# MLP gate and up products by Strassen's scheme, down products behind all of them, zero-state products dropped

## The chip, the cores and the metric

The kernel runs on one core of one Trainium2 chip. The core has TensorE (matmuls into PSUM), VectorE, ScalarE and GpSimd (element-wise work), SyncE (which mostly issues DMA transfers), 16 DMA engines, an on-chip SBUF and a PSUM of 8 banks of 512 float32 columns. The metric is the device time of one launch in microseconds.

## The reference, cut to what matters

A stack of three blocks over `x` (1024 tokens x 1024 features, float32): an S5 and a gMLP block, an SSD and retention block with an MLP, and an mLSTM and long convolution block. The change is in the second and third:

```python
    # second block: y_ssd and y_ret come from chunked scans, 8 chunks of 128 tokens
    x = x + jnp.einsum("bse,ed->bsd", mixed, w_out[i])
    h = rmsnorm_2(x, norm2_w[i])
    a = jax.nn.silu(jnp.einsum("bsd,df->bsf", h, w_gate[i]))   # 1024 -> 2816
    u = jnp.einsum("bsd,df->bsf", h, w_up[i])                  # 1024 -> 2816
    x = x + jnp.einsum("bsf,fd->bsd", a * u, w_down[i])        # 2816 -> 1024

def chunk_state_scan(states, decay):
    def step(carry, inp):
        s, d = inp
        return (carry * d + s).astype(carry.dtype), carry
    _, prev = lax.scan(step, jnp.zeros_like(states[0]), (states, decay))
    return prev
```

The mLSTM of the third block carries its state `C` from zero over 8 chunks in the same way. In all three mixers the state that the first chunk reads is zero, and nothing reads the state that the last chunk leaves.

## The kernel before

Activations lie turned, features on the 128 partitions and the 1024 tokens in a row, as 8 slices (`KT`) in `XT`. Every projection is worked out one tile of 128 output features at a time. Both operands are split into a high and a low part of a shorter float format, and three products are summed in PSUM (high x high, high x low, low x high): a tile is 8 slices x 3 parts x 2 token halves = 48 matmuls 128x512, all in `pe_tile` (L445), with the two buffers `PP[0]` and `PP[1]` in turns. GpSimd splits the weights (`split_tile`, L412 and L415), SyncE loads them (`load_tile`, L382), ScalarE and VectorE split the activations into `Hhi`, `Hlo` (`split_hi`, `split_lo`, L587, L594, L596). The order on each engine is written out by hand, and semaphores count finished tiles (`proj_done`), evicted tiles (`psum_free`), split weights (`w_split`) and split activation slices (`h_ready`).

The MLP runs in three groups of 8, 8 and 6 pairs. A pair is a gate tile and an up tile; VectorE evicts both times the norm's factor `nrs` (L2381, L2383), ScalarE applies Silu, VectorE multiplies (L2386), and the result is split into one slice of `AUhi`, `AUlo`. After each group its part of the down product is added to `XT` (8 tiles, `add_tile`, L530). The norm before it (`norm2`) is deferred: tiles of `gu0` start on `XT` times the norm's weight, and the factor of each token is worked out beside them. `add_deferred` is the last stretch of VectorE's work before:

```python
            for k in range(KT):
                if k == KT - 1:
                    low_halves(range(KT // 2))
                add_tile(dve, name, k // 2, k % 2, subchunks=subchunks)
                dve.drain().then_inc(hf_ready, 1)
                if k == KT - 1:
                    low_halves(range(KT // 2, KT))
                square_add(dve, b, k)
```

In the mixers, TensorE's products of a chunk stand between quarters of projection tiles (`part`) so that it has work while VectorE and ScalarE turn a chunk around. In the mLSTM stage VectorE also runs the long convolution, one step of 1.3 us (L1100) per tap and slice, spread over the chunks by `CONV_SLOTS`. After it, `convb_sync`, `convb_pe`, `convb_dve` and `convb_act` run the `ya` projection (its operand `mlstm` comes back from DRAM) beside the norm of the convolution.

## Time and profile before

| | us |
|---|---|
| median of 3 runs | 3804.71 (3803.73 to 3807.9) |
| the profiled execution | 3802.75 |
| its span, first to last instruction | 3801.0 |
| TensorE busy | 3609.1 (95%) |
| VectorE busy | 2117.7 (56%) |
| GpSimd busy | 1013.7 (27%) |
| ScalarE busy | 924.4 (24%) |
| mean granted clock of TensorE | 0.977 of full |

Busy times are shares of the whole span. Successive matmuls overlap in the records, so the time that one costs is the distance between starts, not its own duration. A float32 matmul that isn't of the shorter format shows as two records.

### The profile page before, as it was taken

What the parts mean: (1) busy time and instruction counts of PE and PEld (TensorE: products, weight loads), DVE (VectorE), ACT (ScalarE), POOL (GpSimd) and SP (SyncE); (2) the same over time, 40 slices, a digit from 0 to 9 for tenths busy, and PEclk for the clock granted to TensorE, in tenths of its full rate; (3) what the DMA queues carried; (4) which work ended last, traced back from release to release, by engine and by line L of the source; (5) the groups of instructions that cost most, each with busy time, mean ns of one, the idle gap of its engine ahead of it and who ended that gap; (6) DMA issues with size and microseconds to landing.
All of it is one profiled execution on the core that took longest, in us unless ns stands there. A gap on an engine that the chain in (4) does not pass through costs nothing.

```text
span 3801.0 us, 44173 instructions
## 1 busy us (share of the span) xinstructions
PE 3609.1 (95%) x17330; PEld 2959.7 (78%) x17330; DVE 2117.7 (56%) x2154; ACT 924.4 (24%) x1027; POOL 1013.7 (27%) x457
## 2 busy tenths in 40 slices
PE   6888999999899999998999999999999999998998
PEld 4677888887687887776888888887778888876886
DVE  7687551265762664545421221246469888866646
ACT  3355221121122332311210000113332222224222
POOL 0000443333243322332444444433100000004442
PEclk9899999999899999999999999999999999999998
DMA  3234313352125765643111111114433555563521
GB/s 127 68 90 129 100 49 111 105 162 76 34 79 155 174 159 142 175 113 111 45 50 48 46 50 50 44 49 131 150 128 128 165 161 161 150 199 128 177 94 61
DMA packets 540019, 415.59 MB, mean 109 GB/s; under 512 B 33480, under 2 KB 496712, under 8 KB 539872
## 3 DMA queue, kind: packets, MB, share of 16 engines
q1 hardware_dynamic: 478320, 293.94, 28.1%
q10 hardware_dynamic: 61552, 119.65, 8.4%
q8 instruction: 98, 1.61, 0.2%
q14 instruction: 49, 0.40, 0.0%
HBM read 291.00 MB, written 120.16 MB: 108 GB/s over the span
## 4 chain that ended last, share of the span: by engine, by line
PE 85%; DVE 7%; ACT 2%; DVEq 2%; DMA 2%; issue 1%; SPq 0%; ACTq 0%; POOL 0%; POOLq 0%
PE proj_ps L445 74%; ACT stage L473 1%; DVE Hlo L594 1%; PE mix_ps L1460 1%; DVE AUX L677 1%; PE proj_ps L1471 1%; DVE WORK L1100 0%; PE proj_ps L2171 0%; PE mix_ps L660 0%; DVEq L675 0%; PE mix_ps L698 0%; PE proj_ps L2172 0%; PE mix_ps L2267 0%; PE mix_ps L2186 0%; PE proj_ps L1324 0%
## 5 line engine op out<-in xcount | busy, mean ns | idle before, releaser
L445 PE MATMUL proj_ps<-Hhi,w_hi 128*128 128x512 f32 x4128 | 1321.4, 402 | 117.1 <-DVE Hlo L594 60.4
L445 PE MATMUL proj_ps<-Hlo,w_hi 128*128 128x512 f32 x4128 | 1285.1, 393 | 0.0
L445 PE MATMUL proj_ps<-Hhi,w_lo 128*128 128x512 f32 x4128 | 1281.2, 392 | 0.0
L412 POOL TENSOR_TENSOR w_hi<-w_raw,zero_col 128x1024 fp32r<-128x1024 f32 (+2 forms) x225 | 429.9, 1911 | 2712.6 <-PE proj_ps L445 1577.8
L445 PEld LDWEIGHTS proj_ps<-Hhi,w_hi 128*128 128x128 f32 x4128 | 768.9, 190 | 314.1 <-issue 84.6
L445 PEld LDWEIGHTS proj_ps<-Hhi,w_lo 128*128 128x128 f32 x4128 | 781.2, 189 | 167.5
L445 PEld LDWEIGHTS proj_ps<-Hlo,w_hi 128*128 128x128 f32 x4128 | 781.8, 189 | 166.7
L415 POOL TENSOR_TENSOR w_lo<-w_raw,w_hi 128x1024 fp32r<-128x1024 f32 (+2 forms) x225 | 581.7, 2585 | 32.0
L1100 DVE SCALAR_TENSOR_TENSOR WORK<-WORK,param_cols 128x1024 f32<-128x1024 f32 x240 | 308.3, 1285 | 20.2 <-issue 0.9
L473 ACT ACTIVATE stage<-proj_ps 128x1024 f32<-128x1024 f32 x112 | 130.2, 1163 | 597.0 <-PE proj_ps L445 596.0
L530 DVE TENSOR_TENSOR XT<-XT,proj_ps 128x1024 f32<-128x1024 f32 (+1 forms) x64 | 78.1, 1220 | 328.0 <-PE proj_ps L445 328.0
L2383 DVE TENSOR_TENSOR AUX<-proj_ps,AUX 128x1024 f32<-128x1024 f32 x22 | 27.0, 1225 | 205.5 <-PE proj_ps L445 205.5
L689 ACT ACTIVATE AUX<-XT 128x1024 f32<-128x1024 f32 (+1 forms) x47 | 49.9, 1062 | 336.9 <-DVE XT L530 311.3
L445 PE MATMUL proj_ps<-AUlo,w_hi 128*128 128x512 f32 x352 | 109.8, 393 | 0.0
L445 PE MATMUL proj_ps<-AUhi,w_hi 128*128 128x512 f32 x352 | 109.1, 391 | 0.0
L445 PE MATMUL proj_ps<-AUhi,w_lo 128*128 128x512 f32 x352 | 108.7, 390 | 0.0
L2372 ACT ACTIVATE AUX<-AUX 128x1024 f32<-128x1024 f32 x22 | 23.4, 1062 | 339.1 <-DVE AUX L2381 339.1
L486 DVE TENSOR_TENSOR stage<-proj_ps,AUX 128x1024 f32<-128x1024 f32 x24 | 29.4, 1225 | 134.4 <-PE proj_ps L445 132.3
L540 DVE TENSOR_TENSOR AUX<-AUX 128x1024 f32<-128x1024 f32 x31 | 80.9, 2611 | 31.9 <-ACT AUX L689 31.7
L594 DVE TENSOR_TENSOR Hlo<-WORK,Hhi 128x1024 fp32r<-128x1024 f32 x56 | 84.1, 1534 | 25.4 <-ACT Hhi L587 17.2
L402 DVE TENSOR_TENSOR w_lo<-w_raw,w_hi 128x1024 fp32r<-128x1024 f32 x64 | 78.1, 1222 | 19.8 <-ACT w_hi L396 16.5
L2381 DVE TENSOR_TENSOR AUX<-proj_ps,AUX 128x1024 f32<-128x1024 f32 x22 | 27.0, 1225 | 105.3 <-PE proj_ps L445 105.1
(436 smaller groups left out, 3449.7 us busy)
## 6 DMA issues: line engine op xcount, KB each, us to landing
w_raw<-in_w_in SPq DMA_DIRECT2D x101, 512.0 KB, 4.4
w_raw<-in_sgu_w_in SPq DMA_DIRECT2D x24, 512.0 KB, 3.8
w_raw<-in_w_out SPq DMA_DIRECT2D x24, 512.0 KB, 4.1
w_raw<-in_w_gate SPq DMA_DIRECT2D x22, 512.0 KB, 3.9
w_raw<-in_w_up SPq DMA_DIRECT2D x22, 512.0 KB, 3.8
w_raw<-in_s_w_in SPq DMA_DIRECT2D x16, 512.0 KB, 4.3
WORK<-mid_acs SPq DMA_DIRECT2D x8, 1024.0 KB, 17.2
mid_qkv<-stage ACTq DMA_DIRECT2D x16, 512.0 KB, 4.9
```

The costliest lines, as they stand in the source:

```text
L402: engine.tensor_tensor(wlo[slot][:, :, :], raw[slot][:, :, :], whi[slot][:, :, :].bitcast(F32), ALU.subtract)\
L412: nc.gpsimd.tensor_tensor(whi[slot][:, 0:kt, :], w, zero_col[:, 0:1].unsqueeze(2).to_broadcast([P, kt, P]), ALU.add)
L415: nc.gpsimd.tensor_tensor(wlo[slot][:, 0:kt, :], raw[slot][:, 0:kt, :], whi[slot][:, 0:kt, :].bitcast(F32), ALU.subtract).then_inc(w_split, 1)
L445: mm = nc.tensor.matmul(ps[:, h * HALF:(h + 1) * HALF], a[slot][:, k, :], b[:, at + k, h * HALF:(h + 1) * HALF], start=(k == 0 and n == 0) ...
L473: a = nc.scalar.activation(dst, src, func)
L530: nc.vector.tensor_tensor(x, x, o.unsqueeze(1), ALU.add).then_inc(psum_free, 1)
L540: nc.vector.tensor_tensor(nsq[0], nsq[0], nsq[1], ALU.add).then_inc(S("sq_added"), 1)
L594: m = nc.vector.tensor_tensor(dst, src, part.bitcast(F32), ALU.subtract)
L677: nc.vector.scalar_tensor_tensor(out=nhf[k % 2], in0=XT[:, k, :], scalar=g(k), in1=rstd, op0=ALU.mult, op1=ALU.mult)\
L689: nc.scalar.activation(nsq[1].unsqueeze(1), XT[:, ds(k, 1), :], ACT.Square).then_inc(S("sq_ready"), 1)
L1100: m = nc.vector.scalar_tensor_tensor(out=acc, in0=u[:, j:j + SEQ], scalar=col(f"convb_w{j}", k), in1=acc, op0=ALU.mult, op1=ALU.add)
L1460: mm = nc.tensor.matmul(o, k8(ml_qe)[:, 2 * h + d, :], cx(d, h), start=False, stop=(d == 1))
```

## The change

Each pair's gate and up tiles are taken as one product of a 2x2 block matrix of weights (gate and up by upper and lower half of the 1024 inputs) with a 2x2 block matrix of activations (upper and lower inputs by first and second 512 tokens). Strassen's scheme, in the form with seven products `P1` to `P7` and chained sums, computes it: each product is 4 slices x 3 parts = 12 matmuls 128x512. Three weight-side operands are taken as they are and four are sums (`block_sums`), worked out for every pair on VectorE; three activation-side operands are differences, worked out once per slice as out_ret's tiles finish (`first_difference`, `other_differences`) and held in `AUhi`, `AUlo`. ScalarE makes the high and VectorE the low part of each weight block, seven products ahead; GpSimd has no part in it. Intermediate sums stay in three PSUM banks per pair (two sets): ScalarE copies a bank after `P1`, `P6` and `P5`, and VectorE adds copies and banks after `P2`, `P5`, `P3` and `P4`. `P1` of a pair is moved ahead into the pair before. The result of each pair goes to DRAM (`au`) and is read back and split for the down products, which all stand behind the 22 pairs. In SSD, retention and mLSTM the products with the zero state in chunk 0 and the state update in the last chunk go; the remaining conv steps of the last mLSTM chunk stand behind its output, and SyncE's and VectorE's work around `ya` is in another order. Several semaphores are renamed, since they are now shared by two stages.

```diff
+AU_TILES = (8, 8, 6)
+PAIRS = sum(AU_TILES)
+
+ORDER = [(0, "P1"), (1, "P1")] + [(p, j) for p in range(PAIRS) for j in ("P2", "P6", "P7", "P5", "P1", "P3", "P4") if not (p == 0 and j == "P1")]
+ORDER = [(p + 1, j) if j == "P1" and n > 1 else (p, j) for n, (p, j) in enumerate(ORDER)]
+ORDER = [x for x in ORDER if x[0] < PAIRS]
+TURN = {x: n for n, x in enumerate(ORDER)}
 
 
...
-            for m, n in enumerate((8, 8, 6)):
-                proj(f"gu{m}", "w_gate_2", 0, m * D, 2 * n, "norm2", pair="w_up_2")
+            proj("gu", "w_gate_2", 0, 0, 2 * PAIRS, "norm2", pair="w_up_2")
+            for m, n in enumerate(AU_TILES):
                 h(f"au{m}", n)
+            for m, n in enumerate(AU_TILES):
                 proj(f"down{m}", "w_down_2", 0, 0, 8, f"au{m}", kt=n, row0=m * D)
         if 3 in blocks:
...
-WORK_N = 19 * 1024
+WORK_N = 19 * 1024 + 3584
...
-        CONV_GATES, CONV_FIRST, CONV_SLOTS = 6, 4 * STEPS + 4, (6, 1, 2, 2, 4, 1)
+        CONV_GATES, CONV_FIRST, CONV_SLOTS = 6, 4 * STEPS + 4, (6, 1, 2, 2, 4, 1, 5, 2)
+        LAST_SLOTS = 6
...
-                pe.wait_ge(S("ml_cx_ready"), 4 * c + 1)
                 for h in range(4):
                     o, vx = ml_y[:, h, 0:VW], hd(ml_vx)[:, h, :]
-                    nc.tensor.matmul(o, hd(ml_d)[:, h, :], vx, start=True, stop=False)
-                    for d in range(2):
+                    mm = nc.tensor.matmul(o, hd(ml_d)[:, h, :], vx, start=True, stop=(c == 0))
+                    for d in range(2 if c else 0):
                         mm = nc.tensor.matmul(o, k8(ml_qe)[:, 2 * h + d, :], cx(d, h), start=False, stop=(d == 1))
                 mm.then_inc(S("mx_y"), 1)
...
-                for q in range(4):
+                if c == NCH - 1:
+                    conv(LAST_SLOTS + 1)
+                    tail_lo(dve, 24 + 3 * c + 2)
+                for q in range(4 if c < NCH - 1 else 0):
                     d, pair = q // 2, q % 2
                     dve.wait_ge(S("mx_update"), ML0["update"] + 4 * c + q + 1)
                     for j in range(2):
                         h = 2 * pair + j
                         x = ml_cx[:, (4 * d + h) * VW:(4 * d + h + 1) * VW]
-                        m = fma(out=x, in0=x, scalar=ml_bc[:, HALF + (h + 1) * CH - 1:HALF + (h + 1) * CH], in1=PP[0][:, j * HALF:j * HALF + VW],
-                                op0=ALU.mult, op1=ALU.add)
+                        if c == 0:
...
             conv_store(sp, 6)
-            conv_store(sp, 7)
             for m in range(2):
                 load_tile(sp, "ya", 0, m)
             sp.wait_ge(S("mx_stored"), ML0["stored"] + 16 * NCH)
             operand_load(sp, "mlstm", mos, ks=range(OB))
+            load_tile(sp, "ya", 1, 0)
+            conv_store(sp, 7)
+            operand_load(sp, "mlstm", mos, ks=range(OB, KT))
+            load_tile(sp, "ya", 1, 1)
             sp.wait_ge(S("cb_stored"), 16 * KT)
             sp.wait_ge(S("cn_turned"), 1)
-            operand_load(sp, "mlstm", mos, ks=range(OB, KT))
             sp.dma_start(cn_c, tiles_of("convb")).then_inc(S("cn_in"), 16)
             wait_stored(sp, "zb")
             sp.dma_start(cn_z[:, 0:4, :], tiles_of("zb")[:, 0:4, :]).then_inc(S("cn_z_in"), 16)
-            for m in range(2, 4):
-                load_tile(sp, "ya", m // 2, m % 2)
             sp.wait_ge(h_ready, plan.hb["mlstm"][0] + KT)
             sp.dma_start(cn_z[:, 4:, :], tiles_of("zb")[:, 4:, :]).then_inc(S("cn_z_in"), 16)
...
-                nc.vector.tensor_copy(sd_cd, h16(ea)[:, :, CH - 1])
-                dve.drain()
-                nc.vector.tensor_tensor(g2(ea), g2(ea), x12[:, XBC_C:XBC_C + 2, :].unsqueeze(2).to_broadcast([P, 2, 8, P]), ALU.mult)
                 if c:
+                    nc.vector.tensor_copy(sd_cd, h16(ea)[:, :, CH - 1])
+                    dve.drain()
+                    nc.vector.tensor_tensor(g2(ea), g2(ea), x12[:, XBC_C:XBC_C + 2, :].unsqueeze(2).to_broadcast([P, 2, 8, P]), ALU.mult)
                     dve.wait_ge(S("mx_stored"), 16 * c)
...
-                nc.vector.tensor_tensor(h16(sd_prev), h16(sd_prev), sd_cd.unsqueeze(2).to_broadcast([P, SSD_HEADS, SSD_HD]), ALU.mult)
-                dve.drain()
-                dve.wait_ge(S("mx_update"), c + 1)
-                nc.vector.tensor_tensor(sd_prev, sd_prev, SD_UPD, ALU.add).then_inc(S("ssd_state"), 1)
+                if 0 < c < NCH - 1:
+                    nc.vector.tensor_tensor(h16(sd_prev), h16(sd_prev), sd_cd.unsqueeze(2).to_broadcast([P, SSD_HEADS, SSD_HD]), ALU.mult)
+                    dve.drain()
+                    dve.wait_ge(S("mx_update"), c + 1)
+                    nc.vector.tensor_tensor(sd_prev, sd_prev, SD_UPD, ALU.add).then_inc(S("ssd_state"), 1)
+                elif c == 0:
+                    dve.wait_ge(S("mx_update"), 1)
+                    nc.vector.tensor_copy(sd_prev, SD_UPD).then_inc(S("ssd_state"), 1)
                 dve.wait_ge(S("mx_std"), c + 1)
                 nc.vector.reciprocal(sd_rs, sd_rs)
...
-                    nc.tensor.matmul(o, sd_xdt[:, h * 64:(h + 1) * 64], h16(sd_s)[:, h, :], start=True, stop=False)
-                    mm = nc.tensor.matmul(o, sd_prev[:, h * 64:(h + 1) * 64], h16(sd_bc[c % 2])[:, h, :], start=False, stop=True)
+                    mm = nc.tensor.matmul(o, sd_xdt[:, h * 64:(h + 1) * 64], h16(sd_s)[:, h, :], start=True, stop=(c == 0))
+                    if c:
+                        mm = nc.tensor.matmul(o, sd_prev[:, h * 64:(h + 1) * 64], h16(sd_bc[c % 2])[:, h, :], start=False, stop=True)
...
+        def bank(p, j):
+            a, b, d = ((PP[0][:, HALVES[0]], PP[0][:, HALVES[1]], PP[1][:, HALVES[0]]),
+                       (PP[1][:, HALVES[1]], PS[:, HALVES[0]], PS[:, HALVES[1]]))[p % 2]
+            return a if j == "P2" else d if j in ("P7", "P4") else b
+
+        COPIES = {x: n for n, x in enumerate([x for x in ORDER if x[1] in COPY])}
+        EVICT = dict(P2=1, P5=2, P3=3, P4=4)
+        BASE = 8
...
+        def norm2_dve(dve):
+            hb = plan.hb["norm2"][0]
+            fma = nc.vector.scalar_tensor_tensor
+
+            def first_difference(k):
+                dve.drain()
+                nc.vector.tensor_tensor(d_first, XT[:, k, HALVES[1]], XT[:, k, HALVES[0]], ALU.subtract).then_inc(S("states_or_difference"), 1)
+                dve.wait_ge(S("klag_ps_or_difference_hi"), BASE + 4 * k + 1 - min(k, 3))
+                nc.vector.tensor_tensor(T_lo[AT["P5"]][:, k, :], d_first, T_hi[AT["P5"]][:, k, :].bitcast(F32), ALU.subtract)\
...
+            def other_differences(k):
+                up = XT[:, k + 4, :]
+                g = col("norm2", k + 4)
+                fma(out=d_kept[k], in0=up[:, HALVES[1]], scalar=g, in1=d_first, op0=ALU.mult, op1=ALU.subtract)
+                fma(out=d_third, in0=up[:, HALVES[1]], scalar=g, in1=d_fourth, op0=ALU.mult, op1=ALU.subtract).then_inc(S("states_or_difference"), 1)
+                dve.drain()
+                fma(out=d_fourth, in0=up[:, HALVES[0]], scalar=g, in1=d_kept[k], op0=ALU.mult, op1=ALU.subtract).then_inc(S("states_or_difference"), 1)
+                at = BASE + (3 * k + 1 if k < 3 else 13)
...
+            for k in range(KT - 1):
+                add_tile(dve, "out_ret", k // 2, k % 2)
+                dve.drain().then_inc(hf_ready, 1)
+                square_add(dve, NB2, k)
+                if k >= 4:
+                    first_difference(k - 4)
+                    other_differences(k - 4)
+            first_difference(3)
+            block_sums(dve, 0)
+            for n in range(3):
+                block_lo(dve, n)
+            for k in range(4):
+                dve.wait_ge(hhi_ready, hb + k + 1)
+                fma(out=Hlo[:, k, HALVES[0]], in0=XT[:, k, HALVES[0]], scalar=col("norm2", k), in1=Hhi[:, k, HALVES[0]].bitcast(F32),
+                    op0=ALU.mult, op1=ALU.subtract).then_inc(h_ready, 1)
+            add_tile(dve, "out_ret", 3, 1)
+            dve.drain().then_inc(hf_ready, 1)
+            for k in range(3):
+                second_lo(k, BASE + 10 + k + 1)
+            for k in range(4, KT):
+                split_lo(dve, "norm2", k, XT[:, k, :], col("norm2", k))
+            other_differences(3)
+            square_add(dve, NB2, KT - 1)
+            for n in range(3, 7):
+                block_lo(dve, n)
...
+        def block_lo(dve, n):
+            dve.wait_ge(S("b_or_block_hi"), BASE + n + 1)
+            m = nc.vector.tensor_tensor(A_lo[n % 7], a_source(n), A_hi[n % 7].bitcast(F32), ALU.subtract)
+            m.then_inc(S("zb_or_block_lo"), 1)
+            if ORDER[n][1] == "P4":
+                dve.drain().then_inc(w_split, 2)
...
+            tt(s1, up[:, 0:4, :], up[:, 4:8, :], ALU.add)
+            tt(s3, gate[:, 0:4, :], up[:, 0:4, :], ALU.subtract)
+            dve.drain()
+            tt(s2, s1, gate[:, 0:4, :], ALU.subtract)
+            dve.drain()
+            tt(s4, gate[:, 4:8, :], s2, ALU.subtract).then_inc(S("e_or_sums"), 1)
...
+        def product_pe(pe, n):
+            p, j = ORDER[n]
+            pe.wait_ge(S("zb_or_block_lo"), BASE + n + 1)
+            evicted = lambda p, k: pe.wait_ge(S("ml_or_evicted"), BASE + 4 * p + k)
+            copied = lambda j: pe.wait_ge(S("klag_or_copied"), BASE + COPIES[p, j] + 1)
+            if j in ("P1", "P2", "P7") and p >= 2:
+                evicted(p - 2, dict(P1=3, P2=1, P7=4)[j])
+            if j == "P6":
+                copied("P1")
+            if j == "P5":
+                copied("P6")
+            if j == "P3":
+                copied("P5")
+            if j == "P4":
+                evicted(p, 2)
+            if p < 2 and j in ("P1", "P2", "P7"):
+                pe.wait_ge(psum_free, GU0 + 2)
+            hb = plan.hb["norm2"][0]
...
+                for m, (a, b) in enumerate(((A_hi, 0), (A_hi, 1), (A_lo, 0))):
+                    mm = nc.tensor.matmul(bank(p, j), a[n % 7][:, k, :], b_operand(j, b)[:, k, :],
+                                          start=(j in ("P1", "P2", "P7") and k == 0 and m == 0), stop=(k == 3 and m == 2), skip_group_check=True)
...
+        def au_hi(act, g):
+            hi, _, k = au_place(g)
+            act.wait_ge(hf_ready, AU0 + g + 1)
+            if g < 4:
+                products_done(act, TURN[PAIRS - 1, "P5"])
+            elif g < 16:
+                act.wait_ge(proj_done, GU0 + 2 * PAIRS + 2)
+            else:
+                act.wait_ge(proj_done, plan.p["down1"]["t0"] + 2)
+            nc.scalar.activation(hi[:, k, :], au_in[g % OB], ACT.Copy).then_inc(hhi_ready, 1)
+
+        def au_lo(dve, g):
+            hi, lo, k = au_place(g)
+            dve.wait_ge(hhi_ready, AU0 + g + 1)
...
+                if j == "P4":
+                    evicted(tt(mlp_u[:, first], COPY["P6"], bank(p, "P4"), ALU.add))
+                    dve.drain()
+                    u, r = (mlp_u, nrs) if p else (mlp_u[:, first], nrs[:, first])
+                    tt(u, u, r, ALU.mult)
+                    dve.drain()
+                    dve.wait_ge(S("mlp_silu"), p + 1)
+                    tt(mlp_u, mlp_u, mlp_g, ALU.mult).then_inc(S("conv_or_au_ready"), 1)
+                    dve.drain()
+                if n + 7 < len(ORDER):
+                    block_lo(dve, n + 7)
+                if j == "P4" and p + 2 < PAIRS:
+                    block_sums(dve, p + 2)
+            for g in range(4, 8):
+                au_landed(dve, g)
+            for g in range(4, 8):
+                au_lo(dve, g)
+            for name, g0 in (("down0", 8), ("down1", 16)):
+                for m in range(KT):
+                    if g0 + m < PAIRS:
+                        au_landed(dve, g0 + m)
+                        au_lo(dve, g0 + m)
+                    add_tile(dve, name, m // 2, m % 2)
```

## Rows read from the trace of the kernel before

**Rows 1.** The page, part 1: busy time of each engine over the span.

```profile
PE 3609.1 (95%) x17330; PEld 2959.7 (78%) x17330; DVE 2117.7 (56%) x2154; ACT 924.4 (24%) x1027; POOL 1013.7 (27%) x457
```

**Rows 2.** Table of windows: window, length, busy by engine, granted clock, DMA share, GB/s.

```profile
2200.00:2400.00 200.00, 200.00 (x880) 164.95 (x879) 40.17 (x28) 10.62 (x10) 81.28 (x36) 1.00 0.17 49
```

**Rows 3.** Timeline of VectorE, end of out_ret: start, duration, instructions, idle before.

```profile
1829.02 1.22 DVE L530 TENSOR_TENSOR XT<-XT,proj_ps 128x1024 f32<-128x1024 f32 x1 [5.33 <-PE proj_ps L445]
1831.37 3.21 DVE L540 TENSOR_TENSOR AUX<-AUX 128x1024 f32<-128x1024 f32 x1 [1.13 <-ACT AUX L689]
1834.50 4.86 DVE L596 SCALAR_TENSOR_TENSOR Hlo<-XT,param_cols,Hhi 128x1024 fp32r<-128x1024 f32 x4
1839.90 1.22 DVE L530 TENSOR_TENSOR XT<-XT,proj_ps 128x1024 f32<-128x1024 f32 x1 [0.53 <-PE proj_ps L445]
1841.25 7.39 DVE L596 SCALAR_TENSOR_TENSOR Hlo<-XT,param_cols,Hhi 128x1024 fp32r<-128x1024 f32 x4
```

**Rows 4.** Timeline of GpSimd in the same stretch: the split of one weight tile.

```profile
1829.06 1.89 POOL L412 TENSOR_TENSOR w_hi<-w_raw,zero_col 128x1024 fp32r<-128x1024 f32 x1 [6.46 <-PE proj_ps L445]
1831.10 2.40 POOL L415 TENSOR_TENSOR w_lo<-w_raw,w_hi 128x1024 fp32r<-128x1024 f32 x1
```

**Rows 5.** Groups of VectorE, shapes apart, whole span: busy us, mean ns, idle before.

```profile
L1534 DVE SCALAR_TENSOR_TENSOR WORK<-WORK 128x512 f32<-128x512 f32 x16 | 10.3, 685 | 0.0
L2381 DVE TENSOR_TENSOR AUX<-proj_ps,AUX 128x1024 f32<-128x1024 f32 x22 | 27.0, 1225 | 105.3 <-PE proj_ps L445 105.1 <-issue 0.3
```

**Rows 6.** Chain of work, first SSD chunk: start, duration, what.

```profile
1228.49 2.29 DVE WORK L2094
1232.06 0.70 PE proj_ps L2171 x4
1232.77 0.43 PE proj_ps L2172 x4
1237.15 2.94 PE proj_ps L445 x12
1240.09 1.72 PE mix_ps L2177 x4
1241.81 2.76 PE proj_ps L445 x12
```

**Rows 7.** Chain of work, first retention chunk.

```profile
1491.81 1.09 PE mix_ps L2272 x16
1492.90 1.05 PE mix_ps L2277 x16
1493.97 0.69 DVE WORK L2345
```

**Rows 8.** Chain of work, first mLSTM chunk.

```profile
3021.38 0.64 ACT WORK L1489
3037.77 1.01 ACT stage L473
3038.83 3.04 PE proj_ps L445 x12
```

**Rows 9.** Chain of work, last mLSTM chunk and the way to `ya`.

```profile
3365.38 0.88 PE proj_ps L1471 x4
3374.62 1.28 DVE WORK L1100
3382.70 6.70 DMA mid_mlstm<-WORK
3389.80 6.66 DMA WORK<-mid_mlstm
```

**Rows 10.** Timeline of TensorE, `ya` tiles 0 and 2: in brackets the idle time before.

```profile
3397.96 1.19 PE L445 MATMUL proj_ps<-Hhi,w_hi 128*128 128x512 f32 x2 [7.69 <-DVE Hlo L594]
3402.34 0.62 PE L445 MATMUL proj_ps<-Hhi,w_lo 128*128 128x512 f32 x2
3432.97 1.19 PE L445 MATMUL proj_ps<-Hhi,w_hi 128*128 128x512 f32 x2 [8.96 <-issue]
```

437 lines of the change are left out of this document (326 added, 111 removed).

## The prediction

> **What bounds the kernel now.** I read the page's busy shares first: TensorE is busy 95% of the span, VectorE 56%, ScalarE 24%, GpSimd 27% [rows 1]. An average hides the stages, so next came the table of windows: in the stage that the change rewrites TensorE is busy 200 of 200 us at full clock, VectorE 40, ScalarE 11, GpSimd 81, and DMA moves only 49 GB/s [rows 2]. Nothing waits there; only fewer TensorE columns can shorten it. The VectorE timeline gives the pace: the evictions of two consecutive tiles of 48 matmuls start 10.88 us apart [rows 3], so one 128x512 matmul costs 0.2267 us. Then I read the chain of work where the change touches the mixers [rows 6 to 9] and the idle time of TensorE around the `ya` tiles [rows 10].
>
> **Gate and up products.** Before: 44 tiles of 48, 44 x 10.88 = 478.7 us. After: 22 pairs of 7 products of 12 matmuls = 154 x 12 = 1848 matmuls; at the same pace 418.9 us. A group of 12 with its waits took 2.76 us in the SSD stage [rows 6], against 12 x 0.2267 = 2.72; at 2.74 the 154 cost 422 us. I take a gain of 57, bounds 54 (2.76) and 60 (2.72).
>
> **Can VectorE and ScalarE feed a pair in 19.2 us?** They take over what GpSimd did, on halves of 512. Two-input operations on 512 columns cost 0.69 on VectorE, on 1024 1.22 [rows 5], and a 512 one on ScalarE 0.64 [rows 8]. Per pair VectorE has 7 low blocks, 4 sums, 4 evictions and one multiply at 0.69 = 11.0, and two multiplies at 1.22 = 2.4: 13.5, plus some 2 of drains and semaphores: 15.5 of 19.2. ScalarE has 7 high blocks and 3 copies at 0.64 and a Silu of about 1.1: 7.5. The dense place is `P4`: evict, two full multiplies, low block, sums of the next pair but one, about 7 us, while products finish every 2.74. Each block is split seven products (19 us) ahead, the bank copies have one product between writer and reader, and VectorE has caught up by `P5`. So no stall in the steady state. The GpSimd splits are gone there, and with them the longer VectorE operations: in [rows 3, 4] the add at L540 begins at 1831.37 inside a GpSimd operation that ends at 1833.50, and ends 1.1 us after it. DMA gains 44 transfers of 512 KB in some 660 us, 35 GB/s beside 49 [rows 2]: hidden.
>
> **Entry from out_ret (norm2).** Before there is no gap: the low halves of seven blocks come before the last tile's add [rows 3]. After, VectorE works through more, in order. For k = 4, 5, 6 each iteration has the add (1.22), the wait for the square on ScalarE (1.1), the sum (1.2, or 3.2 beside GpSimd), then the differences: a subtraction, three ScalarE steps (2.3), a low half, three fused operations and two low halves, 6.5 to 7 in all: near 12.5, 11 and 11 us, against a tile period of 10.88. Started at 1807 it ends at 1842. Then `first_difference(3)` 3.8, the four sums 3.0, three low blocks 1.9, four half-width low halves 2.6, and only then the add of tile 7 (1.2), on whose `psum_free` the first product waits: 1854.8. TensorE finished out_ret at 1839.8 [rows 3]: 15 us idle. Behind the add stand three low halves 1.9, four full ones 5.1, the last differences 4.2, a sum 1.25 and a low block 0.7, so `P6` of pair 0 can start at 1868.4; between, TensorE does three products. 28.6 us of wall for 8.2 of work: 20.4 lost. Pair 0 has short loops too (`P5` waits for a copy that waits for an eviction; `P3` follows `P5` directly; the spread waits for the diagonal): 3. The half clock after the idle time is mostly hidden in the second wait, I add 1. Total 24; bounds 12 (if the differences overlap the tiles) and 32.
>
> **Entry into the down products.** Before none. After, once `P3` of pair 21 is done, VectorE has a multiply, an eviction, four low halves of `au`, the last eviction and two multiplies, then four more low halves, while GpSimd splits the first two down tiles (1.89 + 2.40 each, [rows 4]). As in [rows 3, 4], the two engines take turns. From the end of `P3`, which is 2.7 before the last product ends: the first low half is ready at 5.7, the second, after GpSimd's low operation on the second tile, at 9.2, the next two at 10.4 and 11.5; the eviction and the two multiplies of `P4` end at 14.8; then ScalarE's high half (1.06) and four low halves at 1.2 end at 21.0, 18.3 after the last product. The last of the eight steps of down tile 0 (1.36 each) then ends at 20 instead of 10.9, with a little half clock on the way. Loss 10. Bounds: 5 with the same list and no turns, 14 with every VectorE operation blocked by a GpSimd one. The Trainium skill, page "SBUF — State Buffer", section "Who interferes with whom", says that a VectorE instruction with two SBUF inputs and a GpSimd one that reads SBUF exclude each other for the whole instruction. The trace agrees (1.1 us after GpSimd's end, [rows 3, 4]); by that rule this entry costs the 10 taken, by shared bandwidth it would be nearer the 5. The other `au` operands are split a tile ahead: nothing.
>
> **Zero state.** SSD, chunk 0: TensorE waits there for L2097, which stands behind the two multiplies that go (L2094, 2.29, and a small copy): 2.5. Half of the 5.1 us from 1232.06 to 1237.15 goes, 2.4, and some of its half-speed part, 1: together 6. SSD chunk 7: the update of L2177, 1.7 [rows 6]. Retention chunk 0: L2272, 1.09, is on the chain; VectorE then has a copy in place of L2345 and an add, 1.0: 2.1; chunk 7: the update of L2277, 1.05 [rows 7]. mLSTM chunk 0: the 3.5 us of the state product go, but the next tile waits for ScalarE's eviction at 3037.77, behind VectorE's conv steps and statistics [rows 8]: worth 0. Together 11.
>
> **End of mLSTM and `ya`.** In chunk 7 VectorE goes through four state updates and nine conv steps after `yn`, then the last two operations, a 6.7 us store and a 6.7 us load, then the split; TensorE sits idle 7.69 us until 3397.96, and the first nine of its matmuls come at half pace, 2 us more [rows 9, 10]. After, the updates (4 x 0.88 of TensorE) go and nine conv steps move behind the store: the operand lands 10 us sooner. But the nine steps and GpSimd's split of the first two `ya` tiles now stand in front of its low halves, in turns. I take 7.5, bounds 3 and 12. Then 8.96 us idle before `ya` tile 2, ended by nothing that the profile names [rows 10]: in `convb_sync` its weight load stands behind the load of all `convb` tiles and of half the `zb` tiles. It is moved ahead of them, past a store and four operand loads on SyncE's queue; only the mean load `cn_c` becomes later. Worth 9 and 2 of clock: 11, bounds 0 (the later `cn_c` becomes the next wait) and 11.
>
> **The sum.** -57 + 24 + 10 - 11 - 7.5 - 11 = -52.5. The profiled execution took 3802.75 (span 3801.0), 2 under the median 3804.71; taken from the median: 3752.
>
> **Rivals.**
> *No entry stalls* (VectorE hides the differences beside the tiles): for it, VectorE sits idle about 5 us in each out_ret tile before [rows 3]; against, the serial round trips fill just that. -52.5 - 18 = 3734 and lower. 12%.
> *The entries cost double*, the clock falling in them again and again (after 7.69 idle nine matmuls ran at half pace, [rows 10]): +25, 3777. 15%.
> *VectorE or ScalarE becomes the bound of each pair.* My VectorE sum is 15.5 of 19.2. The place is `P4`'s 7 us. It decides from 19.2 + 52.5/22 = 21.6 us a pair, that is 6 us more than summed, beyond which the kernel is slower than before. Against it: the durations of [rows 5], and that GpSimd, which lengthens them, is idle in this stage. At 22.5 a pair: 3825. 6%.
> *Group boundaries cost*: each product ends an accumulation and begins with two or three waits. If 0.15 us is lost on each of 154 (the difference of 2.76 and 2.72 is 0.04, [rows 6]), +23 less what I counted: 3772. 10%.
> *The mixers' part gives nothing* (every freed stretch becomes a wait): 3752 + 29 = 3781. 7%.
>
> **Numbers.** My forecast holds 50%, its own range 3738 to 3768. The range 3730 to 3783 takes in most of the first, second, fourth and fifth rivals and leaves out about 2 in 10. About 0.2% (8 us) is what a measurement of this kernel can tell from no change. Slower: the VectorE rival, 6%; within 0.2%: 2%; faster: 92%.
>
> **What would show it.** Right: 1848 matmuls on a new line at 0.227 spacing and a TensorE busy share of 100% from pair 1 to pair 21, each pair near 19.2 us; one gap of about 15 us and one of 3 at the end of out_ret; gaps of 3 and 4 us in the first down tile; VectorE near 75% in the stage; no 8.96 us gap before `ya` tile 2. Wrong: gaps repeated in every pair, ended by a VectorE low block or a ScalarE copy; no gap at norm2; the idle time before `ya` unchanged; or the `cn_c` load ending a new wait in the middle of the `ya` tiles.

## The result and the profile after

The changed kernel takes 3775.06 us (median of 4 runs, 3770.1 to 3776.66) against 3805.40 (median of 4, 3803.73 to 3807.9): ratio 0.9915, 95% interval 0.9901 to 0.993. The gain is 30 us; 52.5 were forecast. The profiled execution is the fastest of the four, 3770.1 us with a span of 3768.4, and 32.6 us of span are to be explained.

Busy time of the engines over the span after, beside [rows 1]:

```profile
PE 3556.2 (94%) x16966; PEld 2907.2 (77%) x16966; DVE 2331.3 (62%) x2496; ACT 1057.5 (28%) x1264; POOL 808.6 (21%) x369
```

TensorE has 364 instructions and 53 us of busy time less, and is idle some 20 us more: part of what the products save has become waiting. VectorE has 214 us more and GpSimd 205 us less. The table of windows says where TensorE waits: the entry into the products, the pairs, the entry into the down products (columns as in [rows 2]).

```profile
1837.00:1857.00 20.00, 3.00 (x7) 2.45 (x8) 16.77 (x24) 14.33 (x21) 0.00 (x0) 0.56 0.00 0
1906.00:2284.00 378.00, 378.00 (x1635) 307.12 (x1634) 248.85 (x346) 134.67 (x210) 0.00 (x0) 1.00 0.30 84
2290.00:2310.00 20.00, 13.51 (x45) 9.79 (x44) 17.24 (x12) 6.02 (x7) 7.48 (x3) 0.83 0.50 163
```

Between the entries nothing waits: 378 us of 378 busy at full clock, VectorE 66%, ScalarE 36%, GpSimd 0, DMA 84 GB/s. The timeline of TensorE after shows the waits themselves, in brackets with what ended them. The first two rows are `P1` and `P6` of pair 0; then comes the start of the last matmul of the last product; then slices k = 0, 1 and 4 of the first down tile; then k = 0 and k = 6 of `ya` tile 0.

```profile
1854.01 0.77 PE L2638 MATMUL proj_ps<-Hhi,AUhi 128*128 128x512 f32 x1 [17.33 <-DVE XT L540]
1866.67 0.50 PE L2638 MATMUL proj_ps<-Hhi,w_hi 128*128 128x512 f32 x1 [1.27 <-DVE w_lo L2592]
...
2292.77 0.40 PE L2638 MATMUL mix_ps<-AUhi,w_lo 128*128 128x512 f32 x1
2296.37 0.71 PE L455 MATMUL proj_ps<-AUhi,w_hi 128*128 128x512 f32 x2 [3.20 <-DVE AUlo L2703]
2299.59 1.22 PE L455 MATMUL proj_ps<-AUhi,w_hi 128*128 128x512 f32 x2 [0.83 <-DVE AUlo L2703]
2308.39 0.73 PE L455 MATMUL proj_ps<-AUhi,w_hi 128*128 128x512 f32 x2 [2.46 <-DVE AUlo L2703]
...
3372.43 1.19 PE L455 MATMUL proj_ps<-Hhi,w_hi 128*128 128x512 f32 x2 [3.72 <-DVE Hlo L604]
3384.46 0.74 PE L455 MATMUL proj_ps<-Hhi,w_hi 128*128 128x512 f32 x2 [1.63 <-DVE Hlo L604]
```

The two entries are there as forecast, and of the 7.69 and 8.96 us of [rows 10] 3.72 and 1.63 are left. Against the trace of before, the stretch from the last row of out_ret to the sums behind the MLP (2569.47 before, 2549.51 after) took 713.45 us instead of 730.23: 16.8 gained, 23 forecast. The mixers gained 6.4 (11 forecast), the end of mLSTM and `ya` 13.1 (18.5 forecast). A stretch of the SGU stage that the change doesn't touch took 3 us more; in the traces of the twelve kernels below the same stretch lies between 2.0 less and 2.9 more than before.

So three terms are short, 6, 5 and 5 us, and the entries of 24 and 10 are to be tested: are they what the prediction says, VectorE's and ScalarE's order of work?

### The profile page after: what moved, and what is told of

The parts are those of the page before. It is cut to its first block, busy times and chain, and to the rows that moved or that the text cites. A ratio compares the mean times of both kernels' runs of the same rounds, so it can differ in the third digit from the quotient of the medians.

```text
span 3768.4 us, 43785 instructions
## 1 busy us (share of the span) xinstructions
PE 3556.2 (94%) x16966; PEld 2907.2 (77%) x16966; DVE 2331.3 (62%) x2496; ACT 1057.5 (28%) x1264; POOL 808.6 (21%) x369
## 4 chain that ended last, share of the span: by engine, by line
PE 79%; DVE 8%; issue 3%; DMA 3%; ACT 3%; DVEq 2%; SPq 1%; POOLq 1%; POOL 0%; ACTq 0%
PE proj_ps L455 58%; PE proj_ps L2638 6%; PE mix_ps L2638 5%; DVE Hlo L604 1%; ACT stage L483 1%; PE mix_ps L1470 1%; DVE AUX L687 1%; POOLq L424 1%; PE proj_ps L1484 0%; DMA WORK<-mid_acs 0%; PE mix_ps L670 0%; DMA mid_ssd<-WORK 0%; DVEq L685 0%; PE proj_ps L2193 0%; PE mix_ps L2291 0%
## 5 line engine op out<-in xcount | busy, mean ns | idle before, releaser
L455 PE MATMUL proj_ps<-Hhi,w_hi 128*128 128x512 f32 x3552 | 1145.1, 404 | 109.5 <-DVE Hlo L604 55.9
L455 PE MATMUL proj_ps<-Hlo,w_hi 128*128 128x512 f32 x3552 | 1108.6, 394 | 0.0
L455 PE MATMUL proj_ps<-Hhi,w_lo 128*128 128x512 f32 x3552 | 1105.0, 393 | 0.0
L422 POOL TENSOR_TENSOR w_hi<-w_raw,zero_col 128x1024 fp32r<-128x1024 f32 (+2 forms) x181 | 346.3, 1913 | 2891.0 <-PE proj_ps L455 1996.8
L455 PEld LDWEIGHTS proj_ps<-Hhi,w_hi 128*128 128x128 f32 x3552 | 662.1, 191 | 283.6 <-issue 69.8
L455 PEld LDWEIGHTS proj_ps<-Hlo,w_hi 128*128 128x128 f32 x3552 | 674.3, 190 | 144.7
L455 PEld LDWEIGHTS proj_ps<-Hhi,w_lo 128*128 128x128 f32 x3552 | 673.5, 190 | 144.5
L425 POOL TENSOR_TENSOR w_lo<-w_raw,w_hi 128x1024 fp32r<-128x1024 f32 (+2 forms) x181 | 460.0, 2541 | 25.8
L540 DVE TENSOR_TENSOR XT<-XT,proj_ps 128x1024 f32<-128x1024 f32 x64 | 78.1, 1220 | 261.9 <-PE proj_ps L455 261.9
L406 ACT ACTIVATE w_hi<-w_raw 128x1024 fp32r<-128x1024 f32 x64 | 67.7, 1060 | 27.0 <-ACT stage L483 24.2
```

What stands on the lines that cost most here:

```text
L406: nc.scalar.activation(whi[slot][:, :, :], raw[slot][:, :, :], ACT.Copy).then_inc(S("w_hi_ready"), 1)
L422: nc.gpsimd.tensor_tensor(whi[slot][:, 0:kt, :], w, zero_col[:, 0:1].unsqueeze(2).to_broadcast([P, kt, P]), ALU.add)
L425: nc.gpsimd.tensor_tensor(wlo[slot][:, 0:kt, :], raw[slot][:, 0:kt, :], whi[slot][:, 0:kt, :].bitcast(F32), ALU.subtract).then_inc(w_split, 1)
L455: mm = nc.tensor.matmul(ps[:, h * HALF:(h + 1) * HALF], a[slot][:, k, :], b[:, at + k, h * HALF:(h + 1) * HALF], start=(k == 0 and n == 0) ...
L540: nc.vector.tensor_tensor(x, x, o.unsqueeze(1), ALU.add).then_inc(psum_free, 1)
```

## The experiments

**The two halves of the change.** One kernel is the one before with the mixers, mLSTM and `ya` changed, the other the changed kernel with these as before. No code is new; each takes its half of the diff.

*Mixers, mLSTM and `ya` alone:*

> The kernel before with the change's other half alone: zero-state products dropped in the three mixers, mLSTM's last chunk and the loads of `ya` reordered; the MLP is as before. By my prediction this is worth 29.5 us (SSD 7.7, retention 3.15, end of mLSTM 7.5, `ya` 11), ratio 0.9922. By my reading of the changed kernel's trace it is 6.4 in SSD and retention, 5.5 ahead of `ya` and 7.6 in it, 19.5 us, ratio 0.9949, with one stall of 1.63 us left at tile 1 of `ya` and two of 1.1 us beside the last gate tiles. Rival, that it gives nothing by itself: ratio 1.000.

*Strassen's products alone:*

> The changed kernel with the mixers, mLSTM and `ya` as before: Strassen's products and the down products behind all pairs alone. By my prediction 23 us (57 for the products, less 24 at the entry and 10 at the down products), ratio 0.9940. By my reading of the changed kernel's trace the products give 51 and the entries take 22 to 24 and 10, so 17 us, ratio 0.9955. Rival, the two halves of the change share a gain or a loss: the two ratios of this run and of the one with the mixers alone don't multiply to 0.9915.

Measured: 3786.0 us, ratio 0.9945 (0.9929 to 0.9962), and 3792.49 us, ratio 0.9964 (0.995 to 0.9978). The product of the two is 0.9909, the whole change has 0.9915: if the halves share or spoil something, it is less than these intervals can show (some 6 us each way for one ratio). The first is worth 21 us, not 29.5; the second 14, not 23; both forecasts lie outside the intervals. Both halves fall short, as the trace said.

**Where an operand lies.** In the changed kernel a pair takes 19.44 us, not 7 x 2.72 = 19.04. The starts of the products show which are slow: here `P3`, `P4`, `P2` and `P6`, timeline of TensorE after.

```profile
2114.22 0.39 PE L2638 MATMUL proj_ps<-Hhi,w_hi 128*128 128x512 f32 x1
2116.94 0.39 PE L2638 MATMUL proj_ps<-AUhi 128*128 128x512 f32 x1
2119.70 0.39 PE L2638 MATMUL proj_ps<-Hhi,AUhi 128*128 128x512 f32 x1
2122.50 0.39 PE L2638 MATMUL mix_ps<-Hhi,AUhi 128*128 128x512 f32 x1
```

`P3` takes 2.72 us for its 12 matmuls, `P4` 2.76, `P2` 2.80; `P6`, `P7` and `P5` take 2.80 too, and `P1` 2.76. No boundary between groups costs this: it is spread over all 12, and `P3` is free of it. Nor do the other engines: in the last pair `P7` keeps 0.2333 us a matmul while VectorE, ScalarE and GpSimd stand still (2281.7 to 2286.2). But for `P1`, the slow ones are those that read AUhi or AUlo. The down tiles, which read them as well, run at 0.2289 in both kernels, beside 0.2267 for tiles on Hhi. What sets these two buffers apart is what stands ahead of them: a table of 2112 bytes a partition, 64 more than a multiple of 128, and some small ones. (No trace shows an address; that AUhi and AUlo begin 64 bytes off a multiple of 128 supposes that the small ones fill up to one.)

```diff
-        PC = sb("param_cols", [P, KT, NROWS])
...
         AUX = sb("AUX", [P, WORK_N - 2 * KT * SEQ])
+        PC = sb("param_cols", [P, KT, NROWS])
```

> The changed kernel with one line moved: the table of parameter columns (2112 bytes in a partition, 64 more than a multiple of 128) is declared behind AUhi and AUlo instead of ahead of them, so that these begin at a multiple of 128 bytes as Hhi and the weight tiles do. Theory, placement: a matmul that takes an operand from a buffer that begins 64 bytes off is slower; then P2, P6, P7 and P5 fall from 0.2333 us a matmul to 0.2267, P4 from 0.2300, and the down tiles on AUhi from 0.2289; 88 products x 12 x 0.0066 is 7.0, P4 0.9, the down tiles 1.5, some 9 us in all, ratio to the kernel before 0.989, pair period 19.04 us instead of 19.44. Rival, the pace belongs to the products (their bank, the engines beside them): period 19.44, no gain.

Measured: 3760.16 us, ratio 0.988 (0.9863 to 0.9896), clear of the changed kernel's interval. `P2`, `P7` (with `P6` between them), and then `P1`, `P3` and `P4` with this one line moved:

```profile
2102.72 0.39 PE L2638 MATMUL proj_ps<-Hhi,AUhi 128*128 128x512 f32 x1
...
2108.16 0.39 PE L2638 MATMUL proj_ps<-AUhi,w_hi 128*128 128x512 f32 x1
...
2113.60 0.39 PE L2638 MATMUL mix_ps<-Hhi,w_hi 128*128 128x512 f32 x1
2116.32 0.39 PE L2638 MATMUL proj_ps<-Hhi,w_hi 128*128 128x512 f32 x1
2119.04 0.39 PE L2638 MATMUL proj_ps<-AUhi 128*128 128x512 f32 x1
```

Every product takes 2.72, the pair 19.04, as expected, and the down tiles 0.2267. From the first product to the last matmul of the last it is 430.6 us instead of 438.8.

Is it the place of the product's own operand alone? A second kernel swaps two of the seven slots for weight blocks:

```diff
+        for A in (A_hi, A_lo):
+            A[1], A[5] = A[5], A[1]
```

> The changed kernel with two of the seven operand slots swapped: P1's block of the weights in AUhi and AUlo, P2's in w_hi and w_lo. If the place of the operand sets the pace, P1's matmuls go from 0.230 us to 0.2333 and P2's from 0.2333 to 0.2267, and the time stays within 1 us. If it is the product's PSUM bank, its turn in the pair or the engines beside it, both keep their pace.

In part. `P1`, now with its weights in AUhi, took 2.80 us (0.2333 a matmul) as expected, and `P2`, now in w_hi, 2.73 (0.2275). But three products whose operands had not moved changed as well: `P7` and `P5` from 2.80 to 2.76 and 2.75, `P3` from 2.72 to 2.75. The pair came to 19.35 us. So the place sets the pace, but not by the product's own two operands alone; what else enters stays open, and so does whether 128 bytes is the grid that counts. The one time (3780.18) says nothing at this size.

The same line moved in the kernel before:

> The kernel before with the same line moved as in the aligned run: AUhi, AUlo and the mixers' work space begin at a multiple of 128 bytes. Theory, placement costs a matmul time wherever such an operand is read: the down tiles go from 0.2289 us to 0.2267, 1056 x 0.0022 = 2.3 us, and the mixers some more; ratio 0.998 to 0.9994. If the aligned run's gain had been of the kernel as a whole and not of these operands, this one gains as much as it did: ratio 0.9965.

3803.92 us, ratio 0.9998 (0.9988 to 1.0008). The down tiles went to 0.2267 as expected, 2.3 us of 3800, and no more can be seen. The misplaced buffers were there all along. They cost little while only the down products' moving operand lay in them; Strassen's scheme put weight blocks or differences of 110 of the 154 products there.

**The two entries.** At the first, VectorE is busy 16.77 of 20 us while TensorE waits, and its only gaps of any size are waits of 2.06 us for ScalarE in `first_difference`, one for k = 2 and one for k = 3. The kernel fills them and puts one block's split earlier:

```diff
@@ norm2_dve, first_difference(k)
+                if k == 2:
+                    for n in range(3):
+                        block_lo(dve, n)
+                if k == 3:
+                    block_sums(dve, 0)
@@ norm2_dve
             first_difference(3)
-            block_sums(dve, 0)
-            for n in range(3):
-                block_lo(dve, n)
```

(ScalarE's halves of these splits move with them, and block 3's goes ahead of the last differences.)

> The changed kernel with the entry into the products reordered, no work added or left out: the split of the first three weight blocks and the four block sums of pair 0 are put into the two 2.07 us waits of VectorE for ScalarE's first differences 2 and 3, and the split of block 3 ahead of the last low parts. Theory, VectorE's chain holds P1 and P6 of pair 0: from the last product of `out_ret` to P1 the 17.33 us idle fall by the 4.1 us of filled waits, and P6 (30.6 us after the end of `out_ret`) comes 4.1 + 2.6 = 6.7 us earlier, so the kernel is 4 to 7 us faster than the changed one, ratio to the kernel before 0.990. Rival, the idle time is ScalarE's or a transfer's: P1 starts within 1 us of where it did and nothing is gained.

3773.39 us, ratio 0.9915 (0.9898 to 0.9933): no gain that can be told from none. The theory of what holds `P1` is right, the gain went elsewhere. TensorE (`P1`, the first two matmuls of `P5`, and the window of `P5`, columns as in [rows 2]), then VectorE, then ScalarE of this kernel:

```profile
1852.79 0.77 PE L2642 MATMUL proj_ps<-Hhi,AUhi 128*128 128x512 f32 x1 [13.77 <-DVE XT L540]
1874.12 0.76 PE L2642 MATMUL proj_ps<-AUhi,w_hi 128*128 128x512 f32 x1 [2.86 <-issue]
1874.68 0.63 PE L2642 MATMUL proj_ps<-AUlo,w_hi 128*128 128x512 f32 x1
...
1874.10:1880.00 5.90, 5.28 (x12) 3.79 (x12) 1.45 (x3) 1.52 (x4) 0.00 (x0) 0.58 0.33 86
```

```profile
1869.49 0.69 DVE L2614 TENSOR_TENSOR WORK<-stage,WORK 128x512 f32<-128x512 f32 x1
1870.27 0.69 DVE L2596 TENSOR_TENSOR AUlo<-w_raw,AUhi 128x512 fp32r<-128x512 f32 x1
1871.10 0.69 DVE L2596 TENSOR_TENSOR AUlo<-stage,AUhi 128x512 fp32r<-128x512 f32 x1
1871.71 0.68 DVE L2725 TENSOR_TENSOR AUX<-WORK,proj_ps 128x512 f32<-128x512 f32 x1
```

```profile
1872.42 0.60 ACT L2672 ACTIVATE WORK<-mix_ps 128x512 f32<-128x512 f32 x1 [8.36 <-DVE AUX L2725]
1872.91 0.62 ACT L2592 ACTIVATE AUhi<-WORK 128x512 fp32r<-128x512 f32 x1
1873.43 0.59 ACT L2672 ACTIVATE WORK<-proj_ps 128x512 f32<-128x512 f32 x1
```

The wait before `P1` fell by 3.56, and `P6` starts without one, 5.1 us sooner after out_ret than in the changed kernel (6.7 expected). But `P5` waits 2.86 for ScalarE's copy of `P6` (1873.43), which stands behind its copy of pair 1's `P1` (1872.42), which had waited 8.36 us for the first eviction (L2725, 1871.71), which stands behind the sums of pair 1 (L2614 is the last) and two splits. Even so, `P5` starts 35.7 us after the last row of out_ret, against 39.3 in the changed kernel: the 3.6 us are still there. They go in `P5` itself. Its 12 matmuls start 0.43 us apart, at a granted clock of 0.58, where the changed kernel's, after a wait of 1.21, start 0.23 apart; `P3` starts only 1.3 us sooner. From the last row of out_ret to the last product's last matmul it is 455.4 us instead of 456.7. So the wait that was left cost its own length and 2.3 us of pace. Its length alone doesn't settle this: in the next kernel the wait before `P5` is 1.22, as good as in the changed one, and its matmuls start 0.33 apart on the mean.

At the second entry GpSimd and VectorE are to be kept apart:

```diff
+                    if n == "down0":
+                        for m in range(8):
+                            if m == 1:
+                                pool.wait_ge(h_ready, AU0 + 8)
+                            split_tile(pool, n, m // 2, m % 2)
```

> The changed kernel with one wait more: GpSimd splits weight tile 1 of the first down group only when the first eight low parts of the MLP's output are done, so it doesn't run beside VectorE's low parts. Theory, the two engines hold each other up: the pair of low parts that took 6.04 us takes 2.35, the first down tile starts 1.5 us earlier and its k = 4 up to 3.7 us earlier, unless the transfer of part 4 is late; 2 to 4 us in all, less what tile 1 loses when its split comes late (it ends some 4.3 us after the eighth low part). Rival, the low parts take 3 us each by themselves: 6.04 stays and nothing is gained.

3773.55 us, ratio 0.9918 (0.9901 to 0.9935): nothing. GpSimd's split of tile 1 and the low parts of `au` on VectorE in the changed kernel, then the low parts in this one, and TensorE in this one:

```profile
2293.25 1.89 POOL L422 TENSOR_TENSOR w_hi<-w_raw,zero_col 128x1024 fp32r<-128x1024 f32 x1 [0.82 <-PE mix_ps L2638]
2295.28 3.17 POOL L425 TENSOR_TENSOR w_lo<-w_raw,w_hi 128x1024 fp32r<-128x1024 f32 x1
```

```profile
2293.50 6.04 DVE L2703 TENSOR_TENSOR AUlo<-stage,AUhi 128x1024 fp32r<-128x1024 f32 x2
2299.46 2.35 DVE L2703 TENSOR_TENSOR AUlo<-WORK,AUhi 128x1024 fp32r<-128x1024 f32 x2
```

```profile
2297.70 2.34 DVE L2703 TENSOR_TENSOR AUlo<-stage,AUhi 128x1024 fp32r<-128x1024 f32 x2
2299.97 2.34 DVE L2703 TENSOR_TENSOR AUlo<-WORK,AUhi 128x1024 fp32r<-128x1024 f32 x2
```

```profile
2299.05 0.70 PE L455 MATMUL proj_ps<-AUhi,w_hi 128*128 128x512 f32 x2 [1.76 <-DVE AUlo L2703]
2309.36 0.93 PE L455 MATMUL proj_ps<-AUhi,w_hi 128*128 128x512 f32 x2 [4.56 <-DVE AUlo L2703]
2310.09 1.05 PE L455 MATMUL proj_ps<-AUlo,w_hi 128*128 128x512 f32 x2
2318.05 0.73 PE L455 MATMUL proj_ps<-AUhi,w_hi 128*128 128x512 f32 x2 [1.32 <-POOL w_lo L425]
```

The turns are shown: 6.04 us fell to 2.34 without GpSimd beside them. k = 4 comes 12.5 us after the last product's last row (2296.90) instead of 15.6. But from that last row to the sums behind the MLP both kernels take the same, 256.8 and 256.7 us. Two things eat the 3.1 us. k = 0 to 3 came sooner too, so the wait before k = 4 grew from 2.46 to 4.56, and behind it the matmuls start 0.43 us apart: k = 4 and 5 take 2.44 and 2.02 us instead of 1.49 and 1.37, 1.6 in all. And tile 1, split late, ends a new wait of 1.32.

**The `ya` part alone.** The kernel before with only the loads and the low parts around `ya` in their new order (the diff of `convb_sync` and of its VectorE part).

> The kernel before with nothing but the changed order of loads around `ya`: weight tiles 2 and 3 and the second half of the mLSTM operand ahead of the wait for the convolution's mean, and VectorE's low parts ahead of the diagonal. My prediction gave this 11 us (8.96 of wait and 2 of half clock), ratio 0.9971; by the changed kernel's trace it is 7.6, ratio 0.998, with a wait of some 1.6 us left at tile 1. Rival, without the earlier end of mLSTM the operand comes no sooner and a wait of 3 us or more stays: ratio 0.999 or above.

3792.92 us, ratio 0.9969 (0.9954 to 0.9983), which includes both 11 and 7.6. Locally: `ya` starts 2.80 us earlier than in the kernel before, which is what it had when it came there (2.77), and the last products start 9.65 earlier: 6.9 for the part. TensorE, `ya` tile 0 and the wait that is left:

```profile
3395.16 1.19 PE L445 MATMUL proj_ps<-Hhi,w_hi 128*128 128x512 f32 x2 [7.66 <-DVE Hlo L594]
3407.89 0.73 PE L445 MATMUL proj_ps<-Hhi,w_hi 128*128 128x512 f32 x2 [1.16 <-DVE Hlo L594]
```

The first wait is untouched (7.66), the one of 8.96 gone, one of 1.16 (slice k = 6 of tile 0) and one of 0.56 before it new. (The expectations speak of a wait at tile 1; it stands inside tile 0.) It needs nothing of the earlier end of mLSTM: the rival is out.

**Versions that put these together.** The first has the aligned buffers, the reordered entry and the hold, with the wait only for four low parts (`AU0 + 4`) and the arrival of part 4 noted ahead of VectorE's last multiply.

> Aligned buffers, the reordered entry and GpSimd's split held until four low parts are done, with the fifth part's arrival noted ahead of VectorE's last multiply. Aligned is worth 13 us by its ratio (0.9880 against 0.9915), the entry 4 to 7, the hold with the earlier note 4 to 6: ratio to the kernel before 0.9855, and it beats both kernels. Rival, the gains overlap or go to the wait for part 4's transfer: ratio 0.988.

3762.89 us, ratio 0.9896 (0.988 to 0.9913): no better than the aligned one, 16 us from the expectation by the ratio and 6 from its rival. (In the traces the stretch from the last row of out_ret to the sums behind the MLP is 703.0 us, against 705.3 in the aligned one.) Both entries had waits left, `P5` 3.34 us and k = 4 6.75, each with matmuls at half pace behind it, and in both an engine that works in order was held by something less urgent. The next version moves those:

```diff
-            block_sums(dve, 1)
+                if (p, j) == (0, "P2"):
+                    block_sums(dve, 1)
@@ at P4 of the last pair, ahead of its add, multiplies and store
+                        for g in range(4, 8):
+                            au_landed(dve, g)
+                        for g in range(4, 8):
+                            au_lo(dve, g)
```

> The best so far with two orders changed. VectorE makes the block sums of pair 1 behind the eviction of pair 0's P2 instead of ahead of it, and at the end of the last pair ScalarE and VectorE split parts 4 to 7 of the output ahead of that pair's last add, multiplies and store. Theory, both engines work in order, and what the reordered entry gained stood behind the block sums (P5 of pair 0 waited 2.86 us), what the hold gained behind the multiplies and the store (k = 4 of the first down tile came 14.65 us after the last product begins its last matmul and waited 6.75 us). Then P5 waits under 0.5 us, k = 4 comes 10 us after the last product, and the kernel is 5 to 7 us faster than the best so far: ratio to the kernel before 0.988, span some 3753 us. Rival, part 4's transfer is late by itself (its landing is 4.0 us after the issue, and other loads run beside it): k = 4 stays within 1 us of 14.65 and only the 2.8 us of the entry are gained.

3755.61 us, ratio 0.9864 (0.9847 to 0.988). It beats both kernels, but `P5` still waited 2.67 us and k = 4 came 12.9 us after the last row of the products, not 10. Both times the item moved had only changed places with another: ScalarE's copy of `P6` now stood behind a split that waited for the moved sums, and VectorE took note of all four arrivals (the last at 2298.8) before it made the first low part. The third version mends just these:

```diff
@@ mlp_act
-                if n + 7 < len(ORDER) and (p, j) != (1, "P1"):
+                if n + 7 < len(ORDER) and (p, j) not in ((1, "P1"), (0, "P2")):
+                    if (p, j) == (0, "P6"):
+                        block_hi(act, n + 6)
                     block_hi(act, n + 7)
@@ mlp_dve, P4 of the last pair
                         for g in range(4, 8):
                             au_landed(dve, g)
-                        for g in range(4, 8):
-                            au_lo(dve, g)
+                            if g != 5:
+                                au_lo(dve, g if g == 4 else g - 1)
+                        au_lo(dve, 7)
```

> The last version with two orders mended. At the entry ScalarE's copy of P6 stood behind the split of a block whose sums VectorE made later (the copy began at 1875.03, the split at 1874.50 had waited 2.44 us); the split now stands behind the copy. At the down products VectorE noted the arrival of all four parts before it made the first low part, which began 4.9 us after its high part was done; it now makes each low part one arrival later at most. Theory: the wait of 2.67 us ahead of P5 falls below 0.5, k = 4 of the first down tile comes 8 to 9 us after the last product's last matmul begins instead of 12.9, with waits between k = 4 and 7 that give 1 to 2 us of it back; 4 to 6 us in all, span some 3752, ratio 0.985. Rival, parts 5 to 7 land late by themselves (their high parts began 3.3, 4.5 and 5.9 us after part 4's): k = 4 comes earlier and k = 5 to 7 don't, and the down entry gains under 1.5 us.

3748.35 us (3748.2 to 3751.41), ratio 0.9863 (0.9846 to 0.9879); span 3746.7, 10.7 less than the second version's. TensorE at both entries (`P1` and `P3`; the last row of the products; k = 0, 4 and 5 of the first down tile):

```profile
1853.07 0.77 PE L2642 MATMUL proj_ps<-Hhi,AUhi 128*128 128x512 f32 x1 [13.76 <-DVE XT L540]
1874.78 0.47 PE L2642 MATMUL proj_ps<-Hhi,w_hi 128*128 128x512 f32 x1 [0.83 <-DVE w_lo L2596]
...
2280.32 0.39 PE L2642 MATMUL mix_ps<-AUhi,w_lo 128*128 128x512 f32 x1
2282.29 0.70 PE L455 MATMUL proj_ps<-AUhi,w_hi 128*128 128x512 f32 x2 [1.58 <-DVE AUlo L2712]
2288.66 0.73 PE L455 MATMUL proj_ps<-AUhi,w_hi 128*128 128x512 f32 x2 [0.66 <-DVE AUlo L2712]
2292.00 0.74 PE L455 MATMUL proj_ps<-AUhi,w_hi 128*128 128x512 f32 x2 [1.67 <-DVE AUlo L2712]
```

`P5` doesn't wait, `P3` waits 0.83; k = 4 comes 8.3 us after the last row of the products. From the last row of out_ret to the sums behind the MLP it is 691.6 us, against 713.5 in the changed kernel and 701.0 in the second version. These 9.4 us are more than the 4 to 6 expected, and the pace is the reason at the first entry: counted from out_ret, `P5` starts 2.9 us sooner than in the second version, `P3` 5.1, because the matmuls of `P5` start 0.24 us apart and no longer 0.44. The medians differ by 7.3 us between the second and third version, their ratios hardly (each has its own runs of the kernel before, 3804.15 and 3801.72), so it is the waits in the trace that show the step.

**Chunk 0 of SSD.** Counted from the start of the SSD stage, the sums of squares of chunk 0 come 4.9 us earlier in the changed kernel than before, and those of chunk 1 only 3.4. In the one with the mixers alone it is 5.5 and then 0.9 *later*. The chain of work after, at chunk 1:

```profile
1251.63 11.05 DMA mid_ssd<-WORK
1262.71 1.24 DVE WORK L2114
...
1264.08 0.45 PE proj_ps L2193 x4
```

VectorE's L2114 overwrites what chunk 0's store reads, and the store takes 11.05 us. The same store took 6.7 us in the kernel before, and nobody waited for it. To test this, the last version gets its SSD chunk 0 back as it was:

```diff
+            nc.vector.memset(sd_prev, 0.0).then_inc(S("ssd_state"), 1)
...
-                if c:
-                    nc.vector.tensor_copy(sd_cd, h16(ea)[:, :, CH - 1])
+                nc.vector.tensor_copy(sd_cd, h16(ea)[:, :, CH - 1])
...
-                    if c:
-                        mm = nc.tensor.matmul(o, sd_prev[:, h * 64:(h + 1) * 64], h16(sd_bc[c % 2])[:, h, :], start=False, stop=True)
+                    mm = nc.tensor.matmul(o, sd_prev[:, h * 64:(h + 1) * 64], h16(sd_bc[c % 2])[:, h, :], start=False, stop=True)
```

> The last and fastest version with one part of the change undone: chunk 0 of the SSD mixer has its zero-state product, its two VectorE operations and its state update back, as in the kernel before; all else is as it was. Theory: dropping them moves chunk 0's store 1 to 5 us earlier, it then lands 11 to 13 us after its issue instead of 6 to 7 because a 1 MB load and two of 512 KB run beside it, and VectorE waits for it in chunk 1, so the 5.0 to 5.6 us that chunk 0 gains are lost again, and 0.5 to 2.7 us more, by chunk 1. Then, measured by the sums of squares of chunks 0 and 1 on TensorE, chunk 0 is later than in the kernel before by as much as the stage began later, chunk 1 too (within 0.5 us, no wait of VectorE for the store), and the span is 1.5 to 2.5 us shorter than with the drop, some 3745. Rival, the wait in chunk 1 comes from something else that stays: chunk 0 gets 5.5 us slower, chunk 1 is where it was or later, and the span grows by up to 5 us.

3747.77 us (3746.34 to 3751.05), ratio 0.9855 (0.9839 to 0.9872), the best median, though not to be told from the last version's; span 3745.0, 1.7 less. Chunk 1 in the last version (VectorE, then TensorE behind it), then the lines on chunk 0's and 1's stores and who waited for them, first of the last version, then of this one:

```profile
1261.03 2.94 DVE L2114 TENSOR_TENSOR WORK<-WORK,param_cols 128x1024 f32<-128x1024 f32 x1 [3.82 <-DMA mid_ssd<-WORK]
1264.12 0.70 PE L2193 MATMUL proj_ps<-WORK 128*64 128x128 f32 x4 [4.89 <-DVE WORK L2114]
```

```profile
  DVE WORK L2114: 3.8, 1
DMA to landing us min/median/max: 6.4/9.6/12.8
```

```profile
DMA to landing us min/median/max: 6.8/6.8/6.8
```

This stage began 5.01 us earlier than in the kernel before; its chunk 0 was 4.65 and its chunk 1 4.65 us earlier. The last version began 0.53 later, had chunk 0 5.04 earlier and chunk 1 2.68 later. So with the drop the way to chunk 1 costs 1.8 us more than without it (1.5 to 2.5 expected). The other traces agree: from the start of the stage to chunk 1's sums the four kernels without the drop are 0.3 to 0.4 us behind the kernel before, eight with it 0.5 to 2.7 behind; only the changed kernel's own trace is 3.4 ahead. There the three loads were issued 1 to 3 us earlier in the stage, so the store met less of them and the wait for it was 2.1 us, not 3.3 to 4.3. And two costs that follow the wait in the other eight are missing. In them the same VectorE operation takes 2.9 us, not 1.2 (in the last version a GpSimd split runs beside it), and TensorE sits idle 4.4 to 5.4 us; in the last version it then comes back at half pace, at a granted clock of 0.50, which costs 2.8 us more. Why the loads were early in that trace is open, and it is the trace of the fastest of the four executions; whether the others kept the 3.4 isn't shown. In eight of nine traces dropping SSD's zero-state product in chunk 0 gained nothing.

## Why the prediction was right, and where its terms were off

The direction, the mechanism and the place of the losses were right; the size was 30 us where 52.5 were forecast. The measured 3775.06 lies outside the forecast's own range (3738 to 3768) and inside the wider one only. It is nearer to the times of three rivals (3772, 3777, 3781) than to 3752, but by chance: none of the three is what happened as a whole. Term by term, in the changed kernel's trace against that of before:

| term | forecast | measured |
|---|---|---|
| gate and up products | -57 | -51.0 (154 x 2.777 = 427.7 for 478.7) |
| entry from out_ret | +24 | +24 (what is left of the 16.8: 51.0 - 10 - 24.2; counted by itself some 25, of the 456.7 us from out_ret to the last product) |
| entry into the down products | +10 | +10 (k = 4 at 2308.39; four steps of 1.36 after 2293.0 would give 2298.4) |
| zero state | -11 | -6.4 (-1.9 in the kernel with the mixers alone) |
| end of mLSTM | -7.5 | -5.6 |
| `ya` | -11 | -7.5 (-6.9 alone) |
| S5 and SGU, not touched | 0 | +3.3 |
| sum | -52.5 | -33.0, the span -32.6 |

**The products.** Mis-sized by 6. The prediction took the pace of the old gate and up tiles, which read Hhi and w_hi, for products of which five in seven read AUhi or AUlo; that the down tiles ran at 0.2289 was in the trace before and not looked at. The rival of group boundaries has neither the size (0.15 us a product, measured 0.057) nor the reason: with the buffers moved no group costs more than 2.72. Placement is shown; its rule is not.

**The entries.** Both confirmed, by the sizes (TensorE was idle 17.33 us before `P1` where 15 were forecast, and `P6` started 30 us after out_ret's end where 28.6 were) and by taking them apart: fill VectorE's gaps and `P1` comes 3.56 us sooner, keep GpSimd away and the low parts take 2.34 us instead of 6.04. This agrees with what the prediction cited of the Trainium skill, page "SBUF — State Buffer", section "Who interferes with whom": in the changed kernel GpSimd's operations end at 2295.14 and 2298.45, and VectorE's two low parts, 1.17 us each by themselves, each end 1.1 us behind them (2296.22 and 2299.53; TensorE starts on the first at 2296.37). But neither edit alone gained time: behind each stood the next item of an engine that works in order, and behind the wait for it TensorE's matmuls came at half pace. The rival that VectorE hides the entries is out. In the one of doubled entries the clock does fall, as it says: in the changed kernel 14 matmuls come at half pace behind the 17.33 us, and some more in the first down tile. But that is within the 34 us of both entries together, and the rival asked for 25 more.

**Zero state.** The step that failed is the 6 us of SSD chunk 0: 3.4 were kept in the changed kernel's trace, and in the other eight with the drop none. TensorE did get there 4.9 us sooner. The prediction followed the chain only up to the freed stretch, not to what the earlier work would meet: a store that lands beside 2 MB of loads. This is the rival "every freed stretch becomes a wait", right for this part. The 1.7 of chunk 7 (measured 1.76) and the 1.05 of retention's chunk 7 (1.05) came true. Retention's chunk 0, forecast 2.1, isn't seen: from the end of SSD to chunk 1 the kernels with the drop and those without it differ by less than each kind does within itself, some 2 us. From chunk 0 to chunk 1 alone it is 21.6 to 22.2 us with the drop and 22.8 to 24.4 without. mLSTM's chunk 0, forecast 0, was a loss: the 3.5 us of the state product became a wait of 3.43 us for ScalarE, as the prediction says, but behind it TensorE's next matmuls come at half pace, and by the end of the chunk the changed kernel is 0.8 us later than before, eight of the other nine with this drop 0.8 to 2.3.

**End of mLSTM and `ya`.** Both smaller than taken, inside their bounds. The wait before `ya` fell from 7.69 to 3.72 and its half-paced matmuls stayed (1.19 in the row), and the last gate tiles now wait twice 1.11 us for ScalarE where before they waited twice 0.24. In `ya` the 8.96 us are gone, as said, but the operand's later parts, whose transfer takes 5.80 us, end a wait of 1.63: the bound moved from the weights to the operand.

**The rival on the slower side**, VectorE as the bound of each pair, is out: 248.85 us of 378, 12.8 us a pair where 13.5 were summed without the drains.

## What to carry to other kernels

When the main engine's work shrinks, cost the new work by rows of the same buffers, not just of the same shape: here five of seven products read buffers 64 bytes off the others' grid, and one moved declaration was worth 8 us by the trace and 13 by the ratios, beside the change's 30. A gain on a chain is worth only what comes before the next item of an in-order engine: after each edit read the new waits, and move the item that stands in front, not the one that waits. Read the pace behind a wait as well: here a wait of 2.86 us cost 2.3 us more in slow matmuls, so a gain that only makes TensorE wait sooner can be lost twice. Work that is dropped also moves a transfer; ask what it will then share the DMA engines with.

## What the runs showed of the hardware

Not expected: with the table of 2112 bytes ahead of AUhi and AUlo, a matmul of 128x512 that reads them had a pace of 0.2289 to 0.2333 us, and 0.2267 in every product with the table behind them. Matmuls behind a wait often start 0.43 us apart instead of 0.23, at a granted clock near 0.5: so behind 2.67, 2.86 and 3.34 us before `P5`, behind 4.56 before k = 4, behind 3.43 in mLSTM's chunk 0 and 4.89 in SSD's chunk 1; behind waits of 1.2 before `P5` it differed from kernel to kernel. A store of 512 KB landed after 6.2 to 6.8 us when it was issued 32 us into the SSD stage, and after 11.1 to 13.3 us when it was issued 5 to 6 us sooner, into the loads of 1 MB and twice 512 KB. And a stage whose code is the same in all kernels differed by up to 4.9 us from one profiled execution to the next, so that effects of 2 us were read from waits and distances, not from spans.
